# Four weight slots of the last layer are kept on chip for both token tiles

## What is computed

```python
h = x @ b_w_in                              # 2304 columns of dilated queries, 256 of memory queries
mix = _dilated_attention(qd, shared_k, shared_v)
mo = _mem_attn(qm, mkv[:, :, 0], mkv[:, :, 1])
y = jnp.concatenate([mix, mo], axis=-1) @ w_out[l]
x = _layer_norm(DN_ALPHA * x + y, ...)
f = _peer(x, peer_w_q[l], ...)              # scores 128 x 128 keys, top 16 of each of 8 heads:
x = _layer_norm(DN_ALPHA * x + f, ...)      # sum over 128 experts of gate * gelu(x . u[e]) * v[e]
```

## Time and profile before

| | us |
|---|---|
| median of 3 runs | 2170.22 |
| lowest, highest | 2162.65, 2189.7 |
| the profiled execution | 2162.53 |
| its span, first to last instruction | 2160.7 |
| TensorE matmuls busy | 1939.3 (90%) |
| VectorE busy | 1317.7 (61%) |
| ACT busy | 838.3 (39%) |
| first gather issued | 695.4 |

### The profile page before, as it was taken

How to read it: one execution, slowest core, us unless ns; L and a number is a source line. 1 busy time by engine, 2 the same in 40 slices (tenths; PEclk the granted TensorE clock), 3 DMA queues, 4 the chain that set the end, 5 groups by cost and what they waited for, 6 DMA issues and landing times.

```text
span 2160.7 us, 23839 instructions
## 1 busy us (share of the span) xinstructions
PE 1939.3 (90%) x7750; PEld 1170.9 (54%) x7750; DVE 1317.7 (61%) x2855; ACT 838.3 (39%) x2336; POOL 571.9 (26%) x544
## 2 busy tenths in 40 slices
PE   8999889999998899878899998889999989787776
PEld 7888658885655565333366544445774445232222
DVE  3668746662345588887733645877455478954444
ACT  1547544442231243334323623333355333433332
POOL 0001100000001334443433343333324434343331
PEclk9999999999999999988999999999999999999999
DMA  6543345553434999999999999999999999999997
GB/s 232 177 155 118 118 166 195 192 179 135 176 127 150 397 410 421 421 421 404 421 421 421 421 421 421 421 421 406 421 421 405 421 421 413 422 414 421 422 421 295
DMA packets 99607, 716.56 MB, mean 332 GB/s; under 512 B 11040, under 2 KB 11168, under 8 KB 13472
## 3 DMA queue, kind: packets, MB, share of 16 engines
q0 software_dynamic: 75584, 545.09, 61.2%
q1 hardware_dynamic: 23472, 168.83, 20.7%
q10 hardware_dynamic: 432, 1.16, 0.1%
HBM read 713.99 MB, written 1.05 MB: 331 GB/s over the span
## 4 chain that ended last, share of the span: by engine, by line
PE 49%; DMA 26%; DVE 11%; issue 4%; ACT 3%; POOL 1%; POOLq 0%; ACTq 0%; DVEq 0%; PEldq 0%
DMA arena<-peer_uv,arena 26%; PE bank L804 23%; PE bank L1226 17%; PE bank L991 9%; DVE arena L2032 3%; POOL arena L1866 1%; ACT arena L1755 1%; DVE arena L1977 1%; DVE arena L1969 1%; DVE arena L2014 0%; DVE arena L1971 0%; DVE arena L2012 0%; DVE arena L2015 0%; ACT arena L1457 0%; DVE arena L1974 0%
## 5 line engine op out<-in xcount | busy, mean ns | idle before, releaser
L1226 PE MATMUL bank<-arena 128*128 128x512 f32 x2048 | 990.1, 622 | 179.0 <-ACT arena L1755 178.4
L2032 DVE SCALAR_TENSOR_TENSOR arena<-arena,x_tok 128x1024 f32<-128x1024 f32 x512 | 619.5, 1226 | 498.0 <-DMA arena<-peer_uv,arena 494.4
L1866 POOL DMA_INDIRECT arena<-peer_uv,arena x512 | 552.3, 1079 | 895.0 <-PE bank L1226 812.2
L1226 PEld LDWEIGHTS bank<-arena 128*128 128x128 f32 x2048 | 377.7, 196 | 680.7 <-issue 341.1
L1748 ACT ACTIVATE arena<-arena 128x1 f32<-128x1 f32 x512 | 103.3, 202 | 849.7 <-DVE arena L2032 849.1
L804 PEld LDWEIGHTS bank<-xT,weight_ring 128*128 128x128 f32 x1952 | 271.0, 193 | 55.1 <-issue 40.3
L804 PE MATMUL bank<-xT,weight_ring 128*128 128x128 f32 (+1 forms) x1952 | 287.5, 302 | 1.5 <-DVE xT L1890 0.8
L1755 ACT ACTIVATE arena<-arena 128x128 f32<-128x128 f32 x512 | 197.9, 387 | 0.7
L1742 ACT ACTIVATE arena<-const_tile,arena 128x128 f32<-128x128 f32 x512 | 198.1, 387 | 0.0
L804 PE MATMUL bank<-weight_ring,xT 128*128 128x512 f32 (+4 forms) x480 | 163.5, 489 | 3.1 <-ACT xT L1426 1.5
L1426 ACT ACTIVATE arena<-bank 128x512 f32<-128x512 f32 (+7 forms) x147 | 69.6, 494 | 170.4 <-PE bank L804 170.0
(11 more groups left out here) (212 smaller groups left out, 1554.3 us busy)
## 6 DMA issues: line engine op xcount, KB each, us to landing
weight_ring<-weights SPq DMA_DIRECT2D x159, 1024.0 KB, 4.9
arena<-peer_uv,arena POOLq DMA_INDIRECT x512, 14.7
row_ring<-rows_in POOLq DMA_DIRECT2D x10, 512.0 KB, 5.1
const_tile<-consts POOLq DMA_DIRECT2D x1, 1849.0 KB, 9.2
x_tok<-x_in SPq DMA_DIRECT2D x2, 512.0 KB, 4.7
memT<-memT_in POOLq DMA_DIRECT2D x1, 1024.0 KB, 10.3
row_ring<-rows_in ACTq DMA_DIRECT2D x2, 512.0 KB, 11.4
x_out<-x_tok SPq DMA_DIRECT2D x2, 512.0 KB, 5.4
```

Of the source, the lines that this page charges most:

```text
L1226: ins = pe.matmul(b[:, :], diag[n % DIAGS], gbuf[n % GBUF][:, 1, h * 512:(h + 1) * 512], start=n % P == 0, stop=n % P == P - 1)
L1866: pool.indirect_dma_start(gbuf[n % GBUF].rearrange("p a d -> p (a d)"), None, peer_uv, bass.IndirectOffsetOnAxis(ap=expert[t][:, s:s + 1]. ...
L2032: dve.scalar_tensor_tensor(u, u, 1.0, x[:, t, :], ALU.mult, ALU.mult, accum_out=hdot[:, s:s + 1])\
```

## The change

The two slots of the memory queries and the last two of the output product's eight leave the ring's list of both tiles, which becomes 52 slots each. They stand once, as two pairs, at the end of the weights in memory, and GpSimd loads them before the first gather: the memory queries' pair over 2048 columns of constants that have had their last use, when the product inside the chunks of the gated attention is drained; the output pair, behind row vector 7 and the last memory value of the second block, over 1024 numbers a partition of the big tile and over the first layer's half of `mem_k` and of `mem_v`. TensorE reads them there in both tiles, and waits once for each load. To make room, a tile's dilated queries share three places of three blocks in turn instead of having six. The constants are put in another order, so that those that are spent lie together.

```diff
@@ the list of slots (weight_slots) @@
-    layer += slots_of_columns(bw[:, 2304:]) + slots_of_columns(q)
-    layer += slots_of_rows(a["w_out_2"][1]) + slots_of_columns(a["peer_w_q_2"][1])
+    layer += slots_of_columns(q)
+    layer += slots_of_rows(a["w_out_2"][1])[:NK - 2] + slots_of_columns(a["peer_w_q_2"][1])
     out += layer * NT
...
+    out += [np.zeros((P, SLOT), np.float32)] * (len(out) % PAIR)
+    out += slots_of_columns(bw[:, 2304:]) + slots_of_rows(a["w_out_2"][1])[NK - 2:]
...
@@ places @@
+        spent_consts = where["g_mix"][0]
+        assert spent_consts + PAIR * SLOT <= where["dil_mask1"][0]
+        kept_w = cst[:, spent_consts:spent_consts + PAIR * SLOT]
...
-        dqT = area(24016, 18, P)
+        dqT = area(24016, 9, P)
+        kept_out = [[area(25168, 2 * 512)[:, 512 * h:512 * h + 512] for h in range(2)],
+                    [m[:, 0].rearrange("p a s -> p (a s)") for m in (mem_k, mem_v)]]
...
@@ TensorE, out_step @@
-                w = next_weights()
+                if k < NK - 2:
+                    w = next_weights()
+                elif o == 0 and k == NK - 2:
+                    pe.wait_ge(sem("kept_out_loaded"), 48)
                 for h in range(2):
...
-                    mm(b[:, :], tile_mixT[:, k, :], w[:, h * 512:(h + 1) * 512], k == 0, k == NK - 1, end=k == NK - 1)
+                    part = w[:, h * 512:(h + 1) * 512] if k < NK - 2 else kept_out[k - NK + 2][h]
+                    mm(b[:, :], tile_mixT[:, k, :], part, k == 0, k == NK - 1, end=k == NK - 1)
...
@@ TensorE, dil_score @@
-                        mm(b[:, at:at + nk], dqT[:, u * 3 + g, :], dkT[:, u, 0:nk], True, True, end=g == gs[-1])
+                        mm(b[:, at:at + nk], dqT[:, u % 3 * 3 + g, :], dkT[:, u, 0:nk], True, True, end=g == gs[-1])
...
@@ TensorE, step "qm" @@
-                        block_of((f"qm1_{what[0]}", 0), what[1], 2, tile_xT)
+                        o, i = what
+                        if o == 0 and i == 0:
+                            pe.wait_ge(sem("kept_loaded"), 16)
+                        key = (f"qm1_{o}", 0)
+                        b = begin(key) if i == 0 else bank(key)
+                        for k in range(NK):
+                            mm(b[:, i * P:(i + 1) * P], kept_w[:, i * SLOT + k * P:i * SLOT + (k + 1) * P], tile_xT[:, k, :],
+                               k == 0, k == NK - 1, end=(i == 1 and k == NK - 1))
...
@@ ACT, step "dil_q" @@
-                        blocks((f"dil_q_{o}_{u}", 0), dqT[:, 3 * u:3 * u + 3, :], 3)
+                        blocks((f"dil_q_{o}_{u}", 0), dqT[:, u % 3 * 3:u % 3 * 3 + 3, :], 3)
...
@@ GpSimd @@
             for r in range(NROW, 10):
+                if r == NROW + 3:
+                    wait_drained(pool, ("gla_intra", 0))
+                    pool.dma_start(kept_w, weights[n_slots - 2, :, :]).then_inc(sem("kept_loaded"), 16)
                 pool.wait_ge(sem("rows_used"), r - NROW + 1)
                 load_row(pool, r)
+                if r == 7:
+                    wait_drained(pool, ("mem_value0", 2 * len(MEM_UNITS) - 2))
+                    last = weights[n_slots - 1, :, :]
+                    pool.dma_start(area(25168, 1024), last[:, 0:1024]).then_inc(sem("kept_out_loaded"), 16)
+                    for i, m in enumerate((mem_k, mem_v)):
+                        pool.dma_start(kept_out[1][i], last[:, 1024 + 512 * i:1536 + 512 * i]).then_inc(sem("kept_out_loaded"), 16)
```

More of the change, by code:

```diff
@@ L479, in weight_slots @@
     layer = slots_of_columns(kv[:, :768]) + list(v.transpose(0, 2, 1, 3).reshape(6, P, SLOT))
-    layer += slots_of_columns(bw[:, 2304:]) + slots_of_columns(q)
-    layer += slots_of_rows(a["w_out_2"][1]) + slots_of_columns(a["peer_w_q_2"][1])
+    layer += slots_of_columns(q)
+    layer += slots_of_rows(a["w_out_2"][1])[:NK - 2] + slots_of_columns(a["peer_w_q_2"][1])
     out += layer * NT
-    pad = -len(out) % PAIR
-    w = np.zeros((len(out) + pad, P, SLOT), np.float32)
+    out += [np.zeros((P, SLOT), np.float32)] * (len(out) % PAIR)
+    out += slots_of_columns(bw[:, 2304:]) + slots_of_rows(a["w_out_2"][1])[NK - 2:]
+    w = np.zeros((len(out), P, SLOT), np.float32)
     for n, s in enumerate(out):
@@ L522, in constant_columns @@
     rel = P + i - j
+    put("gla_b", a["a_b_gate_2"][0].reshape(GH, GDK).T)
+    for n in "kv":
+        put("pos_" + n, a[f"cmp_pos_{n}"][0].reshape(16, 2 * HD).T)
+        put("w2_" + n, a[f"cmp_{n}_w2"][0].reshape(2, P, HD).transpose(1, 0, 2))
+    put("w_gate2", a["a_w_gate2_2"][0])
+    put("pT", a["p"][0, 0].reshape(S, 2, P).transpose(2, 1, 0))
     m1 = [np.where((rel >= 0) & (rel <= 128), 0, NEG), np.where((rel >= 0) & (rel % 4 == 0), 0, NEG),
@@ L527, in constant_columns @@
     put("iota", np.broadcast_to(np.arange(PK), (P, PK)))
-    put("gla_b", a["a_b_gate_2"][0].reshape(GH, GDK).T)
-    for n in "kv":
-        put("pos_" + n, a[f"cmp_pos_{n}"][0].reshape(16, 2 * HD).T)
-        put("w2_" + n, a[f"cmp_{n}_w2"][0].reshape(2, P, HD).transpose(1, 0, 2))
-    put("w_gate2", a["a_w_gate2_2"][0])
     put("keysT", a["peer_sub_keys_2"].transpose(3, 0, 1, 2))
-    put("pT", a["p"][0, 0].reshape(S, 2, P).transpose(2, 1, 0))
     return cols
```

## The result

| | kernel before | changed kernel |
|---|---|---|
| median of 12 runs, us | 2165.88 | 2156.69 |
| lowest, highest | 2161.27, 2189.7 | 2150.78, 2160.51 |
| the profiled execution | 2162.53 | 2156.78 |
| its span | 2160.7 | 2155.0 |

The ratio is 0.995, with a 95% interval of 0.993 to 0.9971: 10.8 us gained, between 6.3 and 15 (9.2 us by the medians). 2157 us and 7.5 us had been forecast.

The account below looks back on a forecast made before the run. TensorE was taken to bound the first 700 us and tile 1 up to 1676 us, DMA tile 0 and tile 1 afterwards. Gains of 5.0 + 0 + 2.5 - 0 = 7.5 us gave 2155.0, stated as 2157 us, range 2149 to 2172.

Parts of the forecast that it names:

- The size: Whole kernel: 7.5 us gained, 2155.0 us at the profiled level, given as 2157 us.
- the sum: Whole kernel: 5.0 us from tile 0, 0 and 2.5 us from tile 1, less 0 for added costs: 7.5 us.
- Tile 0, both pairs: Tile 0's steps, about 1060 to 1300 us: DMA sets the time, two removed pair loads worth 5.0 us.
- chain of long gathers: Sign in tile 0: chain still of long gathers, at 421 GB/s, TensorE's waiting down from 9.1 us towards 4.
- Rival 2: Tile 0: TensorE's pace decides there too, one pair in two pays at most; 2157.5 or 2160 us; chance 0.20.
- Tile 1, the query pair: Tile 1's first query step: TensorE sets the time, so the removed load is worth 0, bounds 0 and 2.5 us.
- Rival 1: Both tiles: all four removed loads pay, 10.0 us gained, 2152.5 us; chance 0.12.
- Tile 1, the output pair: Tile 1's output steps, behind 1676 us: DMA sets the time, the removed load worth 2.5 us, bounds 0 and 2.5.
- The kept loads in front: First part, 601 to 670 us: 5.0 us of added transfer falls into 50 us of idle DMA time, cost 0.
- Operands from other places: Matmuls reading kept slots from the constants or mem_k: same time as from the weight ring, cost 0.
- TensorE's stretch in tile 1 as long as before: Sign in tile 1, up to 1676 us: TensorE's stretch keeps its length while the DMA rate dips deeper.

Follow-up runs that it names:

- again: The changed kernel timed and traced once more, no edit: median 2157.85 us beside 2163.72 for the kernel before, ratio 0.997.
- front7: Changed kernel with the first kept pair loaded 8 times instead of once, 7 MB more in the first part: median 2158.93 us, ratio 0.9971 to the kernel before.
- before_again: The kernel before, unchanged, timed and traced a second time: ratio 0.9998 to the kernel before.
- t1_only: Changed kernel with the change undone in tile 0, which loads its four slots from the ring: 2162.97 us, ratio 0.998 to the kernel before.
- t1_query: Changed kernel with only tile 1's memory-query pair kept, the other three pairs from the ring: 2165.34 us, ratio 1.001 to the kernel before.
- t1_out: Changed kernel with only tile 1's output pair kept, the other three pairs from the ring: 2161.97 us, ratio 0.9989 to the kernel before.
- before_shift: Kernel before with each tile's last VectorE block of expert numbers computed 20 gathers later: median 2164.31 us, ratio 0.9994 to the kernel before.
- t0_only: Changed kernel with the change undone in tile 1, which loads its four slots from the ring: 2161.73 us, ratio 0.9972 to the kernel before.
- shift: Changed kernel with each tile's last VectorE block of expert numbers computed 20 gathers later: median 2154.73 us, ratio 0.996 to the kernel before.
- drop_t0: Changed kernel with tile 0's dilated queries taking 6 slots instead of 18, results altered: median 2145.11 us, ratio 0.993 to the kernel before.
- drop_t1: Changed kernel with tile 1's dilated queries taking 6 slots instead of 18, results altered: median 2153.81 us, ratio 0.9963 to the kernel before.
- shift_again: Changed kernel with each tile's last VectorE expert-number block 20 gathers later, timed and traced again: median 2154.2 us, ratio 0.9938 to the kernel before.

## Why the prediction was right, point by point

**The size.** 7.5 us forecast, 10.8 and 6.5 us measured, with 7.5 in both intervals; 2157 us forecast and 2156.69 measured. The level chosen between the profiled execution and the median of three was luck in part: with more runs the median before fell from 2170.22 to 2165.88 us. There is luck in the 7.5 as well. From the first gather to the last the three traces of the changed kernel (changed, again, front7) take 1432.5 to 1433.0 us and the two of the kernel before 1436.1 and 1437.7, which is only 3.1 to 5.2 us. In these five traces the two places of the sum gain 7.3 us on average, as follows, but 256 to 330 is 2.0 us longer and 0 to 144 is 1.3 us longer; the sum had no term for either.

**Tile 0, both pairs: 5.0 us.** Held. The six traces in which tile 0 loads its slots from the ring (before, before_again, t1_only, t1_query, t1_out, before_shift) have 348.0 to 351.1 us in 144 to 256, mean 349.7; the seven with kept slots in it and all its queries 343.4 to 345.9, mean 344.9. That is 4.7 us. TensorE's waits in exactly these gathers, in the kernel before and after:

```profile
PE bank L1226 <- ACT arena L1755: 31.1, 26, 2.8
```

```profile
PE bank L1232 <- ACT arena L1772: 26.2, 21, 2.8
```

31.1 us become 26.2 in these two traces. Over the groups it is less: the six traces without kept slots in tile 0 have 27.8 to 31.2 us of this waiting, mean 29.5, the seven with them 26.1 to 28.6, mean 27.3. That is 2.2 of the 4.7 us. Another 2.2 us are gone from TensorE's busy time (318.4 to 316.2 us on average) for the same matmuls; that these are matmuls at the lower clock behind waits is my reading. The rate is 420 or 421 GB/s in all thirteen. I had said that the waiting in 1080 to 1260 us would fall from 9.1 us towards 4, and that did not come: it is 7.2 to 9.1 us in five traces (again, front7, changed, t0_only, shift). That step was read over the wrong stretch: the later part of the tile holds most of the waiting. The sign "chain of long gathers" could not be read, since the chain of the changed kernel's trace does not reach back to this tile.

**Rival 2, tile 0 as tile 1.** Not here, but not far: drop_t0 shows that a further 14.9 us would gain 9.3.

**Tile 1, the query pair: 0.** Held, by drop_t1 (six loads less in the same stretch, and 118.34 us from gather 292 to 330 as with all of them) and by t1_query's 473.3 us. Rival 1, that all loads pay, is out by the same numbers.

**Tile 1, the output pair: 2.5 us.** Held in size; where it is gained is shown only with both tiles' slots kept. Without it 330 to 511 takes 473.2 to 475.1 us in five traces (before, before_again, before_shift, t0_only, t1_query), mean 473.9; with it and without the shift 470.6 to 473.2 in seven (changed, again, front7, t1_only, t1_out, drop_t0, drop_t1), mean 471.4: 2.6 us. With both tiles' slots kept (changed, again, front7) the gain stands where the load was, 195.6 to 196.7 us in 330 to 400 against 198.4 to 199.2 in the four traces without the pair and without the shift. In t1_only and t1_out it does not; there it is gather 402 that is less late. Whether the missing load does that too, further on, or chance, no run tells.

**The kept loads in front: 0.** Held, by front7. The prediction's word that TensorE never waits for a load there is right, though the earlier trace rows show SyncE's waits only: in 540 to 700 us of the kernel before TensorE's longest wait is 1.8 us, for VectorE, and none is for a load.

**Operands from other places: 0.** Held. The output steps' matmuls of 512 columns in 1650 to 1700 us (count, busy us, mean ns) take the same from the ring and from all three kept places:

```profile
L810 PE MATMUL bank<-weight_ring,xT 128*128 128x512 f32 x24 | 11.3, 592 | 0.0
L810 PE MATMUL bank<-arena,xT 128*128 128x512 f32 x4 | 1.9, 592 | 0.0
...
L810 PE MATMUL bank<-mem_k,xT 128*128 128x512 f32 x2 | 1.0, 592 | 0.0
L810 PE MATMUL bank<-mem_v,xT 128*128 128x512 f32 x2 | 1.0, 592 | 0.0
```

The query blocks from const_tile take 275 ns a matmul, as in the earlier trace rows.

**TensorE's stretch in tile 1 as long as before.** This step missed something that the sum had no term for. The changed kernel's waits in 1480 to 1671 us, against the earlier trace rows:

```profile
PE bank L1232 <- ACT arena L1772: 5.0, 2, 3.5
```

and the longer of them in the timeline (start us, us, engine, line):

```profile
1522.10 1.22 DVE L2058 SCALAR_TENSOR_TENSOR arena<-arena,x_tok 128x1024 f32<-128x1024 f32 x1
...
1523.37 0.20 ACT L1765 ACTIVATE arena<-arena 128x1 f32<-128x1 f32 x1 [6.72 <-DVE arena L2058]
...
1524.21 0.50 PEld L1232 LDWEIGHTS bank<-arena 128*128 128x128 f32 x2 [3.71 <-ACT arena L1772]
...
1527.78 2.98 PE L810 MATMUL bank<-xT,weight_ring 128*128 128x128 f32 x16
...
1528.80 0.94 POOL L1892 DMA_INDIRECT arena<-peer_uv,arena  x1 [7.73 <-PE bank L1232]
```

VectorE's product for the gather is held up by its block of expert numbers (1515.74 to 1522.10 us), ACT's diagonal comes after it, and TensorE waits 3.52 us; the four matmuls that follow take 3.78 us and the block behind them 2.98 us, in place of 1.88 and 1.95. The gather behind it is released 9.1 us after the last, 5.6 us late, and the next another 1.0 us late. The kernel before has one such wait too, at 290 in one trace and at 274 in the other, the one that the prediction was read from:

```profile
1474.18 3.78 PE L1226 MATMUL bank<-arena 128*128 128x512 f32 x4 [3.05 <-ACT arena L1755]
```

It stands 6 us ahead of the window 1480 to 1676 us in which the earlier trace rows count a single wait of 1.5 us. In the traces 256 to 330 takes 235.7 to 237.4 us with the wait at 290 (232.4 in t1_query) and 230.7 to 232.9 with it at 274. I had taken one execution's stretch for the kernel's. What decides between 274 and 290 is open. The kernel before shows both, the changed one 290 in its three traces with all loads, which is too few to say that the change has no part in it; many traces of each kernel would tell, and this wasn't tried.

## What to carry to other kernels

A load that is taken out of a full queue is worth its transfer time only where that queue sets the pace, and two engines within 7% of each other take turns: read the chain at each place where something is removed, not over the pass. An event that every trace has in the same order, like the n-th gather, shows in which stretch 2 to 5 us are gained where the times of whole executions can't; but two traces of the same kernel are needed before a difference is called the change's, and a stretch is best cut once more, to see whether the gain stands where the change is. And a long VectorE block that stops TensorE can be worth moving: here 3.5 to 5.5 us between the first gather and the last of the changed kernel, and nothing clear in the kernel before (0.9994), where the wait stood behind another block.

## What the runs showed of the hardware

One execution of the shifted kernel took 2174.11 us and was traced; its gathers take 1427.5 us as in the others, but the first goes out at 715.6 us in place of 693.3. Windows 90 to 100, 100 to 120 and 150 to 160 us of that trace, and then of shift (the clock is the third number from the end):

```profile
90.00:100.00 10.00, 10.00 (x67) 10.00 (x67) 9.34 (x2) 4.00 (x5) 0.00 (x0) 0.71 0.50 169
100.00:120.00 20.00, 20.00 (x96) 20.00 (x95) 9.42 (x11) 5.27 (x7) 0.00 (x0) 0.50 0.43 147
150.00:160.00 10.00, 10.00 (x65) 9.08 (x65) 6.50 (x21) 0.81 (x2) 0.00 (x0) 0.55 0.01 2
```

```profile
90.00:100.00 10.00, 10.00 (x92) 10.00 (x92) 7.92 (x3) 4.06 (x5) 0.00 (x0) 1.00 0.64 232
100.00:120.00 20.00, 20.00 (x137) 18.42 (x136) 16.51 (x20) 10.91 (x17) 0.00 (x0) 1.00 0.67 248
150.00:160.00 10.00, 9.85 (x67) 8.00 (x65) 6.64 (x11) 6.72 (x17) 0.00 (x0) 1.00 0.51 197
```

TensorE is busy without a gap in all of 90 to 120 us in both, yet the granted clock is 0.71 and then 0.50, which is 1.2 of 2.4 GHz, in the one and 1.00 in the other. It gets through 96 matmuls in the time of 137. What sets it off no row shows: the engine had been busy, 10.00 of every 10 us from 20 us on, before the clock fell. By ACT's instructions, counted off in both traces, shift_again is 1.7 us behind shift at 75 us, 17.8 us at 161 us and 22.3 us at 305 us. The Trainium skill, TensorE: Matmul & The Clock Gate, Part 1: The HAM clock gate, has the clock at half rate when the engine has been idle; the wait of 3.52 us in tile 1 and the slow matmuls behind it agree with that, this fall in the middle of a busy stretch does not follow from it.

The times some 20 us above the rest of a kernel (2174.58 and 2176.44 us in shift, 2189.7 us in the kernel before) may be the same thing; only this one was traced. A smaller form stands in front7, ahead of all its extra loads. Window 260 to 270 us of front7, and then of again:

```profile
260.00:270.00 10.00, 9.09 (x51) 6.01 (x50) 3.47 (x6) 1.19 (x2) 0.00 (x0) 0.50 0.01 2
```

```profile
260.00:270.00 10.00, 9.09 (x56) 5.42 (x53) 3.47 (x6) 1.19 (x2) 0.00 (x0) 0.86 0.01 2
```

As busy, at 0.50 in place of 0.86; the ten microseconds before have 0.67 in place of 0.97. The late first gather of front7 comes from here: the same instruction of ACT starts at 244.8 us in front7 and 247.3 in again, a later one at 344.4 and 339.8, and the first gathers stand at 700.7 and 695.9 us. So nothing is lost from 601 us on, where the extra loads are.

Also new to me: the lower clock after a short wait. A wait of 3.52 us cost 6.6 us in the changed kernel's tile 1, since the matmuls behind it ran at the lower level: the granted clock is 0.51 in 1524 to 1530 us and 1.00 in 1530 to 1533 us.
